# SyncE issues the output weights and the first expert weights after 13 of the 16 ada items of the two summed groups

## The chip, the cores and the metric

The kernel runs on one core of a Trainium2 chip. The metric is device time in microseconds (us), from the first to the last instruction of the program and what lies around it. The kernel before takes 1914.93 us, the median of three runs (1913.94 to 1918.86).

## What is computed

Two blocks run one after the other on 256 tokens of width 1024, all in float32. The first has two layers:

```python
def first_block(x, c, ...):
    cond = silu(c)
    for i in range(2):
        mod = cond @ ada_w[i] + ada_b[i]             # 1024 x 6144: 24 MB of weights per layer
        sh1, sc1, g1, sh2, sc2, g2 = split(mod, 6)
        h = rms_norm(x, norm1_g[i]) * (1 + sc1) + sh1
        y = diff_attention(h, ...) if i == 0 else stick_breaking_attention(h, ...)
        x = x + g1 * y
        h = rms_norm(x, norm2_g[i]) * (1 + sc2) + sh2
        x = x + g2 * hierarchical_moe(h, ...)        # 32 experts, gate, up and down of 2 MB each
    return rms_norm(x, final_norm_g)
```

Each attention has an input product `h @ w_in` (1024 x 3072, six pieces of 2 MB) and an output product `o @ w_out` (two pieces of 2 MB). The second block takes the result and a context through two more layers; its modulation comes from `w_mod_2` in the same way as above.

## The kernel before, in words

**The ring.** SyncE (SP) loads nearly all large weights into a ring of six slots of 2 MB, in one fixed order: for layer `l` the six pieces of the input weights, the two of the output weights (`weight(l, n)`, n = 0 to 7, L1256 to L1269), then gate, up and down of every expert (`expert(l, e)`, L1324 and L1330). Before each load it waits in `room(n)` until the load six places earlier has been used. So the output weights take the slots of the first two input weights, and gate and up of experts 0 and 1 take the slots of the other four; the loads after them need the slots of the output weights. The downs of the first two experts do not lie in the ring in layer 0 and come later, behind another wait (L1284).

**The ada items.** The modulation of both blocks is computed in 64 items, each 1 MB of a modulation matrix: 8 items (one for each eighth of the 1024 rows) make a group of 2048 columns. GpSimd (POOL) loads them, in order, into three buffers (`ada_load`, L1371). Item i is called by its number here; items 0 to 31 are loaded in layer 0, 32 to 63 in layer 1 (32 to 34 a little earlier). Groups 1, 2, 5 and 6 are *summed* (items 0 to 15 and 32 to 47): VectorE (DVE) scales each item by its column of `cond` and adds it to the item before (`ada_sum`, L1699, first item L1701), and TensorE (PE) needs one short product with a column of ones for the eighth item of the group. In the other groups PE multiplies each item itself. The load of item i waits until item i-3 is free: for a summed one that is when item i-2 has been added.

**Counting.** The semaphore `ada_used` counts items in order: DVE raises it for the first seven items of a summed group, PE for all others.

**PE's order.** PE takes the items at fixed places in its program:

```python
QKV_ITEMS = ...                  # item 7 (39) behind step 6 of the input product, item 15 (47) behind step 11, its last
DIFF_ITEMS = share_out(16, [0, 0] + 8 * [1] + [0, 0] + 4 * [1, 0])   # layer 0: items 16 to 23 in steps 2 to 9, ...
if 1 <= k < 9: ada_item(47 + k)  # layer 1: items 48 to 55 in steps 1 to 8 of 18
```

In layer 0, behind item 20 is loaded, POOL also waits until the row of group 2 is stored (`ada_store`, L1389), and issues a bias load, three short column loads and two row loads before it loads item 21; in layer 1 the same stands in front of item 53. After the attention come the output product (`projection`), the router and the experts. In `projection` PE frees the slots of the output weights (L2106), and with that SP goes on.

Of the kernel before, what the change touches and what calls it, by code (L numbers as in the profile page):

```python
# [29 lines left out]
KT = D // P  # L30
# [102 lines left out]
def program(nc, a, out, sb, sem, ctx):  # L133
# [49 lines left out]
    LAST0, LAST1 = 4, 8  # L183
# [143 lines left out]
    def slot(n):  # L327
        return n % RING
# [5 lines left out]
    def free(n):  # L334

        return sem(f"used{slot(n)}")

    def wslot(n, rows_, cols):
        return ring[:, slot(n), :].rearrange("p (t n) -> p t n", t=rows_)[:, :, 0:cols] if cols else None
# [915 lines left out]
    def _(sp):  # L1255
        def room(n):  # L1256

            if n >= RING:
                sp.wait_ge(free(n), n // RING)

        def weight(l, n):

            room(L_BASE[l] + n)
            W = a[loads[l][n]][0]
            if n < 6:
                src = W[:, n * 512:(n + 1) * 512].rearrange("(p t) n -> p t n" if l else "(t p) n -> p t n", t=KT)
            else:
                src = W[:, (n - 6) * 512:(n - 5) * 512].rearrange("(t p) n -> p t n", t=KT)
            sp.dma_start(wslot(L_BASE[l] + n, KT, 512), src).then_inc(sem(f"loaded{slot(L_BASE[l] + n)}"), 16)  # L1269
# [76 lines left out]
        for l in range(2):  # L1346
            for n in range(8):
                weight(l, n)
            for e in range(NX):
                if e == TAIL:  # L1350
                    sp.wait_ge(sem("cnt"), EACH["cnt"] * l + 1)
                    fullest = sp.value_load(most[0:1, 0:1], min_val=0, max_val=S)
                    with sp.If(fullest > LIST):
                        overflow(l)
                expert(l, e)
# [1071 lines left out]
```

## Time and profile before

| | |
|---|---|
| median of 3 runs | 1914.93 us (1913.94 to 1918.86) |
| span of the profiled execution | 1914.1 us; its whole time is not listed apart, and the median lies 0.8 us above this span |
| PE busy | 1697.9 us (89%) |
| DVE busy | 500.2 us (26%) |
| DMA | 586.38 MB, mean 306 GB/s |
| longest chain | PE 54%, DMA 30%, DVE 7% |

Columns of a group of instructions: busy time and mean time of one, then the idle time of the engine before them and what ended most of it. In a timeline a row starts with the start and the duration in us, and the last bracket is the idle time before. q1 is the queue of SP's transfers, q0 that of POOL's; the share of a queue is that of the time of the 16 DMA engines in the stretch. Times are from the start of the span.

### The profile page before, as it was taken

The numbers are of one execution on the slowest core, as the hardware profiler recorded it, in microseconds if no ns is written. First come the engines' busy times: TensorE is split into PE (matmuls) and PEld (weight loads), VectorE is DVE, ScalarE is ACT, GpSimd is POOL, SyncE is SP. The second block draws the span as 40 slices with busy tenths as digits, with TensorE's granted clock in tenths as the row PEclk, the third lists the DMA queues.
The fourth block names the chain that finished last, engine by engine and source line by source line (L and its number), as shares of the span: only waits on it lengthen the run. The fifth ranks groups of instructions, "written<-read, shape, count | busy, mean of one in ns | idle before, by whom it ended". The sixth has DMA issues, their size and how long they took to land.

```text
span 1914.1 us, 18209 instructions
## 1 busy us (share of the span) xinstructions
PE 1697.9 (89%) x7421; PEld 848.8 (44%) x7421; DVE 500.2 (26%) x944; ACT 398.0 (21%) x860; POOL 96.0 (5%) x167
## 2 busy tenths in 40 slices
PE   5967799889898888989989899999999899889988
PEld 3823353333333333845453433333343456555564
DVE  1338331000000103243241000010102334663362
ACT  2003121111111101114231111011100334352351
POOL 1102000000000010123000000000001000000000
PEclk9988899999999989999999999999999899999999
DMA  9997179999999999986369999999999622123310
GB/s 352 389 381 284 45 281 379 422 423 422 423 421 421 421 419 402 379 335 237 115 262 417 424 417 423 418 421 419 419 420 385 237 90 89 57 79 125 111 66 23
DMA packets 122521, 586.38 MB, mean 306 GB/s; under 512 B 10275, under 2 KB 15467, under 8 KB 97849
## 3 DMA queue, kind: packets, MB, share of 16 engines
q1 hardware_dynamic: 99064, 491.94, 63.6%
q0 software_dynamic: 16192, 82.13, 11.5%
q10 hardware_dynamic: 7168, 11.02, 1.5%
q8 instruction: 63, 1.03, 0.2%
q14 instruction: 34, 0.27, 0.0%
HBM read 572.89 MB, written 12.15 MB: 306 GB/s over the span
## 4 chain that ended last, share of the span: by engine, by line
PE 54%; DMA 30%; DVE 7%; ACT 3%; issue 3%; SPq 2%; POOL 0%; ACTq 0%; DVEq 0%
PE psum L2019 51%; DMA ring<-in_expert_w_up 21%; DMA work<-in_ada_w 4%; DMA ring<-in_diff_w_in 2%; DVE work L1699 1%; DMA work<-in_ctx 1%; PE psum L619 1%; DVE small L966 1%; DMA ring<-in_consts 1%; SPq L1324 1%; PE psum L2258 1%; PE psum L1096 1%; SPq L498 1%; DVE work L1911 1%; SPq L1303 0%
## 5 line engine op out<-in xcount | busy, mean ns | idle before, releaser
L2019 PE MATMUL psum<-ring,work 128*64 128x512 f32 (+5 forms) x4432 | 1150.4, 574 | 78.8 <-DMA ring<-in_expert_w_up 64.2
L2019 PEld LDWEIGHTS psum<-ring,work 128*64 128x64 f32 (+2 forms) x4432 | 444.2, 153 | 700.8 <-issue 666.6
L2019 PE MATMUL psum<-work 128*128 128x192 f32 (+8 forms) x920 | 193.5, 378 | 8.1 <-DVE work L1849 4.2
L1911 DVE TENSOR_TENSOR work<-work,psum 128x256 f32<-128x256 f32 x64 | 26.9, 421 | 614.4 <-ACT work L1623 614.4
L2019 PEld LDWEIGHTS psum<-work 128*128 128x128 f32 (+2 forms) x920 | 130.8, 192 | 103.4 <-issue 84.0
L1623 ACT ACTIVATE work<-psum 128x256 f32<-128x256 f32 x64 | 24.5, 383 | 689.1 <-PE psum L2019 689.1
L2019 PE MATMUL psum<-work,ring 128*128 128x256 f32 (+1 forms) x728 | 161.2, 380 | 4.4 <-DMA ring<-in_diff_w_in 1.5
L2019 PEld LDWEIGHTS psum<-work,ring 128*128 128x128 f32 x728 | 136.0, 191 | 29.8 <-issue 7.2
L1502 ACT ACTIVATE work<-psum 128x256 f32<-128x256 f32 (+4 forms) x153 | 69.7, 461 | 229.0 <-PE psum L2258 67.5
L1933 DVE TENSOR_TENSOR work<-psum,rows 128x512 f32<-128x512 f32 x64 | 44.2, 691 | 272.0 <-PE psum L2019 272.0
L1699 DVE SCALAR_TENSOR_TENSOR work<-work,small 128x2048 f32<-128x2048 f32 x28 | 65.8, 2351 | 94.8 <-DMA work<-in_ada_w 94.5
L1502 ACT ACTIVATE ring<-psum 128x512 f32<-128x512 f32 (+3 forms) x82 | 49.9, 608 | 77.0 <-PE psum L2019 56.6
L1571 ACT ACTIVATE work<-psum,small 128x192 f32<-128x192 f32 x128 | 58.4, 506 | 25.2 <-PE psum L2019 25.2
L2019 PE MATMUL psum<-work,cst 128*128 128x256 f32 (+4 forms) x152 | 28.5, 413 | 27.5 <-DVE work L1699 20.0
L1464 POOL DMA_INDIRECT work<-expert_rows,picks x8 | 7.7, 965 | 883.8 <-DMA expert_rows<-work 882.0
L2258 PE MATMUL psum<-cst,work 128*128 128x128 f32 x128 | 28.0, 300 | 17.7 <-DVE work L1911 17.7
L966 DVE TENSOR_REDUCE small<-psum 128x1 f32<-128x512 f32 (+1 forms) x48 | 28.7, 598 | 47.1 <-PE psum L2019 46.9
L619 PE MATMUL psum<-cst 128*128 128x256 f32 x166 | 40.6, 396 | 0.0
L2019 PE MATMUL psum<-work,small 128*2 128x512 f32 (+1 forms) x256 | 37.9, 677 | 2.4 <-DMA work<-in_ada_w 1.8
L839 ACT ACTIVATE ring<-psum,small 128x512 f32<-128x512 f32 (+1 forms) x48 | 29.6, 616 | 41.5 <-DVE small L966 39.8
L1176 PE MATMUL psum<-cst,ring 128*128 128x128 f32 x160 | 27.3, 286 | 11.6 <-DVE ring L972 11.1
L619 PEld LDWEIGHTS psum<-cst 128*128 128x128 f32 x166 | 31.6, 198 | 10.7 <-issue 6.7
(258 smaller groups left out, 817.9 us busy)
## 6 DMA issues: line engine op xcount, KB each, us to landing
ring<-in_expert_w_gate SPq DMA_DIRECT2D x60, 2048.0 KB, 16.7
ring<-in_expert_w_up SPq DMA_DIRECT2D x60, 2048.0 KB, 21.3
ring<-in_expert_w_down SPq DMA_DIRECT2D x57, 2048.0 KB, 21.1
work<-in_ada_w POOLq DMA_DIRECT2D x40, 1024.0 KB, 8.4
ring<-in_w_in SPq DMA_DIRECT2D x12, 2048.0 KB, 9.1
work<-in_w_mod POOLq DMA_DIRECT2D x16, 1024.0 KB, 5.2
ring<-in_diff_w_in SPq DMA_DIRECT2D x6, 2048.0 KB, 37.4
ring<-in_sb_w_in SPq DMA_DIRECT2D x6, 2048.0 KB, 25.0
```

The lines of the kernel that those rows point to most:

```text
L619: nc.tensor.matmul(bank[b][:, 0:S], ident, cst[:, 0:S], start=True, stop=True, skip_group_check=True)
L839: nc.scalar.activation(pe_[:, k % 3, 0:n * P], bank[4 + k % 3][:, 0:n * P], ACT.Exp, bias=nm2[:, k % 3:k % 3 + 1], accum_out=sm2[:, k % 4: ...
L966: V.tensor_reduce(nm2[:, k % 3:k % 3 + 1], bank[4 + k % 3][:, 0:n * P], AX.X, ALU.max, negate=True).then_inc(sem("a_max"), 1)
L1176: ins = T.transpose(bank[(7, 2)[u % 2]][:, j * P:(j + 1) * P], pe_[:, u % 3, j * P:(j + 1) * P], ident)
L1502: copy = lambda o_, i_: nc.scalar.activation(o_, i_, ACT.Copy)
L1571: ins = nc.scalar.activation(hS[:, c // QUAD % 2, t, 0:QUAD * LIST], bank[b][:, k * S:k * S + QUAD * LIST], ACT.Identity, scale=gain[:, t: ...
L1623: nc.scalar.activation(s_act, gu_bank(e)[:, 0:S], ACT.Silu).then_inc(sem("silu"), 1)
L1699: ins = V.scalar_tensor_tensor(now, now, cond[:, 0, t:t + 1], before, ALU.mult, ALU.add)
L1911: V.tensor_tensor(hid, s_act, gu_bank(e)[:, S:2 * S], ALU.mult).then_inc(sem("hid"), 1)
L1933: V.tensor_tensor(outb[:, e % 2, :], bank[5 + e % 2], gate2, ALU.mult).then_inc(sem("out_ev"), 1)
L2019: return T.matmul(out_, lhsT, rhs, start=start, stop=stop, skip_group_check=True)
L2258: ins = T.transpose(bank[2][:, j * P:(j + 1) * P], src[:, j * P:(j + 1) * P], ident)
```

## The change

SP waits once more in each layer, ahead of the first output weight: until 13 items are used in layer 0, and 45 in layer 1 (LAST0 is 4 and KT is 8, so `8 * (4 * l + 2) - 3`).

```diff
         def weight(l, n):

             room(L_BASE[l] + n)
+            if n == 6:
+                sp.wait_ge(sem("ada_used"), KT * (LAST0 * l + 2) - 3)
             W = a[loads[l][n]][0]
```

Everything that SP issues later stands behind this wait: the two output weights, gate and up of experts 0 and 1, and all that follows.

## Rows read from the trace of the kernel before

**Rows 1.** The page: span, and the chain that ended last, by engine.
```profile
span 1914.1 us, 18209 instructions
...
PE 54%; DMA 30%; DVE 7%; ACT 3%; issue 3%; SPq 2%; POOL 0%; ACTq 0%; DVEq 0%
```

**Rows 2.** Waits of the whole span: total, times, longest.
```profile
DVE work L1699 <- DMA work<-in_ada_w: 94.5, 25, 8.8
...
PE psum L2019 <- DVE work L1699: 20.0, 2, 16.4
```

**Rows 3.** Timeline of PE: ends of both input products, and the first output product.
```profile
119.51 7.10 PE L2019 MATMUL psum<-ring,work 128*128 128x512 f32 x16 [0.15 <-PE psum L2019]
143.02 1.89 PE L2019 MATMUL psum<-work,cst 128*1 128x512 f32 x8 [16.41 <-DVE work L1699]
...
211.01 7.13 PE L2019 MATMUL psum<-ring,work 128*128 128x512 f32 x16 [0.69 <-ACT work L1502]
...
854.19 1.04 PE L2019 MATMUL psum<-work,cst 128*1 128x512 f32 x8 [3.56 <-DVE work L1699]
```

**Rows 4.** Timeline of SP: the issues around the change, both layers.
```profile
71.57 15.48 SPq L1269 DMA_DIRECT2D ring<-in_diff_w_out  x2
...
126.65 0.33 SPq L1324 DMA_DIRECT2D ring<-in_expert_w_up  x1
...
778.18 15.79 SPq L1269 DMA_DIRECT2D ring<-in_sb_w_out  x2
806.74 0.34 SPq L1324 DMA_DIRECT2D ring<-in_expert_w_gate  x1
822.26 0.34 SPq L1324 DMA_DIRECT2D ring<-in_expert_w_up  x1
```

**Rows 5.** Windows, two stretches; the last columns are clock, DMA share and GB/s.
```profile
71.60:91.40 19.80, 19.47 (x94) 15.83 (x93) 6.43 (x4) 1.79 (x3) 1.06 (x2) 1.00 1.03 394
...
138.40:164.70 26.30, 16.55 (x99) 6.13 (x100) 22.04 (x50) 8.87 (x38) 8.11 (x15) 0.74 0.80 286
```

**Rows 6.** Waits of SP for the whole span.
```profile
SPq L1324 <- PEq L2106: 112.1, 1, 112.1
```

**Rows 7.** Timeline of POOL: the loads of items 9 and 10, of 41 and 42, of 43.
```profile
91.44 1.74 POOL L1371 DMA_DIRECT2D work<-in_ada_w  x2 [14.26 <-PE psum L2019]
...
815.45 1.74 POOL L1371 DMA_DIRECT2D work<-in_ada_w  x2 [23.21 <-PE psum L2019]
...
823.07 0.55 POOL L1371 DMA_DIRECT2D work<-in_ada_w  x1 [5.30 <-DVE work L1699]
```

**Rows 8.** Items 41 and 42 alone, issued 815 to 817: time to landing.
```profile
DMA to landing us min/median/max: 4.9/6.5/8.1
```

**Rows 9.** Items 11 and 12, issued 102 to 106: time to landing.
```profile
DMA to landing us min/median/max: 11.7/13.7/15.7
```

**Rows 10.** Timeline of DVE: the sums of items 12 and 44.
```profile
121.41 2.35 DVE L1699 SCALAR_TENSOR_TENSOR work<-work,small 128x2048 f32<-128x2048 f32 x1 [4.91 <-DMA work<-in_ada_w]
...
835.24 2.35 DVE L1699 SCALAR_TENSOR_TENSOR work<-work,small 128x2048 f32<-128x2048 f32 x1 [0.15 <-DMA work<-in_ada_w]
```

**Rows 11.** The page, DMA issues: size of each.
```profile
ring<-in_expert_w_gate SPq DMA_DIRECT2D x60, 2048.0 KB, 16.7
...
work<-in_ada_w POOLq DMA_DIRECT2D x40, 1024.0 KB, 8.4
```

**Rows 12.** Timeline of PE: items 21 and 55.
```profile
164.70 1.04 PE L2019 MATMUL psum<-work,small 128*1 128x512 f32 x8 [1.84 <-DMA work<-in_ada_w]
...
890.83 1.04 PE L2019 MATMUL psum<-work,small 128*2 128x512 f32 x8
```

**Rows 13.** Queues in 109.9 to 138.4: packets, MB, share.
```profile
q1 hardware_dynamic: 468, 6.67, 55.1%
q0 software_dynamic: 808, 5.11, 43.8%
```

**Rows 14.** Queues in 112 to 116, when both have work.
```profile
q1 hardware_dynamic: 76, 1.15, 67.5%
q0 software_dynamic: 82, 0.55, 32.7%
```

**Rows 15.** Queue of POOL in 834 to 862.
```profile
q0 software_dynamic: 1136, 5.69, 53.8%
```

**Rows 16.** Queues in 714 to 726, smaller pieces of expert weights beside three items.
```profile
q0 software_dynamic: 368, 2.64, 53.1%
q1 hardware_dynamic: 368, 2.38, 47.9%
```

**Rows 17.** Windows of 5 us at the start of the attention of layer 1.
```profile
850.00:855.00 5.00, 1.44 (x10) 0.11 (x8) 2.35 (x1) 1.88 (x2) 0.00 (x0) 1.00 1.03 429
855.00:860.00 5.00, 2.08 (x13) 1.49 (x10) 2.19 (x5) 2.96 (x6) 2.65 (x5) 0.53 0.97 410
```

**Rows 18.** Timeline of PE: items 48, 49 and 50.
```profile
861.68 1.89 PE L2019 MATMUL psum<-work,small 128*2 128x512 f32 x8
...
868.55 1.20 PE L2019 MATMUL psum<-work,small 128*2 128x512 f32 x8
...
872.40 1.04 PE L2019 MATMUL psum<-work,small 128*2 128x512 f32 x8
```

## The prediction

> **What bounds the kernel now.** I read the page first. The chain that ended last is PE for 54% and DMA for 30% [rows 1], so neither alone bounds the kernel, and the place decides. The view of waits names what the change aims at: PE waited 20.0 us in two places for the summing of ada items on DVE, 16.4 us of it at once, and DVE in turn waited 94.5 us for the items to land [rows 2]. The timeline of PE puts the two places: the input product of layer 0 ends at 126.6 us, and PE stands 16.41 us until item 15 is summed; in layer 1 it stands 3.56 us before item 47 [rows 3]. The timeline of SP shows the competition. The output weights of layer 0 are issued from 71.57 us, and the last of the first expert weights (up of expert 1) at 126.65 us, so six transfers of 2 MB flow beside items 5 to 15 [rows 4]. And the DMA engines are full there: the windows give a share of 1.03 in 71.6 to 91.4, while in 138.4 to 164.7, the first half of the attention, the share is 0.80 [rows 5]. So bytes are what this stage is short of, and the question is whether the change saves bytes ahead of the point that matters, or only moves them.
>
> **The change, part by part.** It adds one wait in each layer and removes nothing. A wait that is met costs a fraction of a microsecond on SP, which is on no chain here. Behind it on SP stand, in each layer, six transfers: two output weights, gate and up of experts 0 and 1. The next one needs the slot that the output product frees, and SP stood 112.1 us for that in layer 0 [rows 6]. So nobody needs the six early: I cost their lateness itself at nothing, covered by the rest of the attention, some 60 us in layer 0. If they landed after 211.01 us they would hold up the output product [rows 3]; by the sums below they land before 170.
>
> *When the wait is met, layer 0.* Items 0 to 8 keep their times, since the group's eighth item has its place in PE's program, behind step 6 of the input product. Loads of items 9 and 10 go out at 91.44 us as before [rows 7]. With no traffic of SP beside them I take layer 1's items 41 and 42, which met almost none: they land 4.9 and 8.1 us after their issue [rows 8], instead of 11.7 to 15.7 us as items 11 and 12 do now [rows 9]. One sum takes 2.35 us [rows 10], a load goes out some 0.3 us after the sum that frees its buffer. Item 9 lands at 96.3 and is summed at 98.7, item 10 at 99.5 and 101.9; item 11 goes out at 99.0, lands 5 us later at 104.0, summed 106.4; item 12 goes out at 102.2, lands 107.2, summed 109.6. That is the thirteenth: SP is released at 109.6 instead of 71.57. Before, the same sum ended at 121.41 + 2.35 = 123.8 [rows 10].
>
> *The wait of 16.41 us.* Item 13 is in flight at 109.6, item 14 just issued, item 15 goes out behind item 13's sum, at about 114.7. Output weights now flow beside them; the nearest row for that has about 8.4 us to landing, as the usual one on the page [rows 11]. So item 15 lands near 123.1 and is summed near 125.5. PE reaches it at 126.6. The wait of 16.41 us is gone, and PE enters the attention at 126.6 instead of 143.0.
>
> *Where the bytes go.* They are now late, and next in line are items 16 to 23, one in each step of the attention. PE took item 21 at 164.70, after 1.84 us of waiting for its landing [rows 12]. Nothing behind that item changes its pace, so its time is the measure of layer 0. The sum is one of engine time. SP still owes 6 x 2.10 MB = 12.6 MB [rows 11]. In 109.9 to 138.4 its queue moved 6.67 MB in 55.1% of 28.5 us, 425 GB/s while it had the engines [rows 13]: 29.6 us. POOL's queue owes items 14 to 21, 8.4 MB, and 0.3 MB of row loads, at 5.11 MB in 43.8% of 28.5 us = 409 GB/s [rows 13]: 21.3 us. If all of SP's goes ahead of item 21, the load of item 21 ends at 109.6 + 29.6 + 21.3 = 160.5. A lone item takes 4.9 us, of which 1.05 MB at 409 GB/s are 2.6, so 2.3 lie around the transfer: it lands at 162.8. **Layer 0: 1.9 us gained**, out of the 16.4.
>
> *Does all of SP's go ahead?* In 112 to 116, with both queues at work, the two moved almost equal numbers of packets, 76 and 82, but 1.15 MB and 0.55 MB [rows 14]: expert weights come in packets twice as large. At one third of the engines, POOL gets only four items through while gate and up of both experts pass. So yes. The Trainium skill says, in "DMA: Bandwidth & Descriptors", section "Queues, rings and completion order", that each engine takes turns between its queues by whole packets, not by bytes; with equal shares of bytes in its place the sum would be rival A's. By that rule, the trace agrees; it speaks against this change.
>
> *Layer 1.* SP issued the output weights from 778.18 us [rows 4]. Now it waits for item 44. Items 41 and 42 go out at 815.45 as before [rows 7] and are summed by 826.5; item 43 (issued 823.07 [rows 7]) without a rival lands at 828.1, summed 830.4, item 44 (issued 826.8) is summed at 834.1, instead of 835.24 + 2.35 = 837.6 [rows 10]. Item 47 then lands near 847 and is summed before PE arrives at 850.6: the 3.56 us are saved. But here SP had issued four of its six transfers by 822.26 [rows 4], in time that was not short, and all six now follow: 12.6 MB, 29.6 us. POOL owes items 46 to 55, the last that stand in consecutive steps: 10.5 + 0.3 MB at 5.69 MB in 53.8% of 28 us = 378 GB/s [rows 15], 28.6 us. 834.1 + 29.6 + 28.6 + 2.3 = 894.6, against 890.83 for item 55 now [rows 12]. **Layer 1: 3.8 us lost**, the saved 3.56 us included.
>
> *Sum.* -1.9 + 3.8 = 1.9 us slower. The span is 1914.1 and the median of the runs 0.8 above it, which I take as what lies around it: 1914.9 + 1.9, about 1917 us. Bounds of the unknown terms: layer 0 between 10.2 us gained (equal shares, rival A) and 1.1 lost, if the engines run at the share of 0.80 of [rows 5] in the last 15 us, where only POOL's loads are left (3 us more); layer 1 between 2.8 us lost and 6.8 lost, by the same two.
>
> **Rival A: POOL keeps half of the engines.** For it: in 714 to 726, beside smaller pieces of expert weights, POOL had 53.1% and moved 2.64 MB against 2.38 [rows 16]. Against it: [rows 14], with the large pieces that flow here. Then layer 0 ends at 109.6 + 21.3 / 0.5 + 2.3 = 154.5, 10.2 us gained; layer 1 at 834.1 + 57.2 + 2.3 = 893.6, 2.8 lost. Sum 7.4 us faster, 1907.5 us.
>
> **Rival B: both waits go and nothing takes their place,** the transfers being hidden in the attention. For it: DMA has a share of 0.80 there [rows 5]. Against it: the free 20% of 26.3 us are 5.3 us of the engines, and SP still owes 29.6 us of them when it is released, of which the rest of the input product covers 17. 20.0 us faster, 1894.9 us.
>
> **Rival C: PE loses its clock in layer 1.** There the attention is PE's own pace, and a stop costs twice. Before, the 3.56 us of waiting and the gap behind them were followed by a granted clock of 0.53, near the lower of its levels of 1.2 and 2.4 GHz [rows 17]; item 48 to item 49 then took 6.9 us where 49 to 50 takes 3.9 [rows 18], 3.0 us lost in a step. If PE stops for each of items 51 to 55, it comes out of the last with two steps at the low clock: 6.0 us on top of the forecast, 1922.9 us. [...] Against it: DMA is the bound up to item 55 anyway, and the full clock may return while it waits. It ends slower than before by more than a measurement tells.
>
> That the wait is met at once and does nothing is excluded in layer 0: SP is at the place at 71.57 and the thirteenth sum is 38 us away, and in layer 1 56 us.
>
> **Chances.** About 0.3%, 5.7 us, is what a measurement of this kernel can tell from no change. The forecast, within that of the time before: 0.47, between 1909 and 1920.6. A: 0.19. B: 0.05, and 0.01 for more. C, and layer 1 at its worse bound with layer 0 at its own: 0.28. So faster 0.25, same 0.47, slower 0.28. The range leaves out B and the tail of C: 1904 to 1925.
>
> **What would show it.** Right: SP issues the output weights near 110 and 834; PE waits under 1 us at item 15 and at item 47; in their place PE waits several times, up to some 6 us each, for landings of items 17 to 21 and 51 to 55; items 17 to 20 need 12 us and more to land; item 21 is taken near 163 and item 55 near 895; the DMA share is close to 1 until 160. The output product starts within 3 us of before in layer 0. Wrong: if item 21 is taken before 157, shares of the queues were mis-sized (A or B); if item 15 is still waited for, the landings beside the output weights were; if the low clock lasts beyond 895, C.

## The result and the profile after

The changed kernel takes 1932.70 us, the median of four runs (1928.85 to 1934.39); the kernel before takes 1916.53 us on the same chip (four runs, 1913.94 to 1918.86). The ratio is 1.0086, 95% interval 1.0070 to 1.0101: slower by some 16 us, where 1917 us had been forecast, 2 us slower. The profiled execution has a span of 1927.0 us, 12.9 more than before; it is the fastest of the four (1928.85), so the rows below hold somewhat less than the 16 us.

The page of the changed kernel, span and busy times; beside [rows 1]:

```profile
span 1927.0 us, 18211 instructions
...
PE 1704.2 (88%) x7421; PEld 850.9 (44%) x7421; DVE 500.2 (26%) x944; ACT 398.2 (21%) x860; POOL 96.0 (5%) x167
```

Timeline of SP: the new wait lets the output weights go at 110.35 and 835.51 us, against 71.57 and 778.18 in [rows 4].

```profile
110.35 0.99 SPq L1271 DMA_DIRECT2D ring<-in_diff_w_out  x2
...
835.51 1.00 SPq L1271 DMA_DIRECT2D ring<-in_sb_w_out  x2
```

Timeline of PE in layer 0: item 15, the items of the first attention steps, and the start of the output product (item 15 and output product of before in [rows 3], item 21 in [rows 12]).

```profile
127.21 1.04 PE L2021 MATMUL psum<-work,cst 128*1 128x512 f32 x8 [0.30 <-PE psum L2021]
...
141.63 1.89 PE L2021 MATMUL psum<-work,small 128*1 128x512 f32 x8 [6.68 <-DMA work<-in_ada_w]
...
149.01 1.88 PE L2021 MATMUL psum<-work,small 128*1 128x512 f32 x8 [3.72 <-DMA work<-in_ada_w]
...
157.62 1.89 PE L2021 MATMUL psum<-work,small 128*1 128x512 f32 x8 [4.31 <-DMA work<-in_ada_w]
...
166.62 1.04 PE L2021 MATMUL psum<-work,small 128*1 128x512 f32 x8 [1.15 <-DMA work<-in_ada_w]
...
212.66 7.13 PE L2021 MATMUL psum<-ring,work 128*128 128x512 f32 x16 [0.69 <-ACT work L1504]
```

The wait of 16.41 us is gone: item 15 follows the input product by 0.30 us. In its place PE waits for items 17, 18 and 19 (6.68, 3.72, 4.31 us) and a little for each up to item 22. Item 21 is taken 1.9 us later than before, and the output product starts 1.65 us later.

The same for layer 1: item 47, then 48, 49, 50, 51 and 55, and the output product. First the output product of the kernel before:

```profile
923.62 7.13 PE L2019 MATMUL psum<-ring,work 128*128 128x512 f32 x16 [0.47 <-ACT work L1502]
```

The changed kernel:

```profile
853.13 1.04 PE L2021 MATMUL psum<-work,cst 128*1 128x512 f32 x8 [0.30 <-PE psum L2021]
...
859.98 1.58 PE L2021 MATMUL psum<-work,small 128*2 128x512 f32 x8
...
871.59 1.89 PE L2021 MATMUL psum<-work,small 128*2 128x512 f32 x8 [7.31 <-DMA work<-in_w_mod]
...
882.71 1.89 PE L2021 MATMUL psum<-work,small 128*2 128x512 f32 x8 [4.29 <-DMA work<-in_w_mod]
...
889.58 1.88 PE L2021 MATMUL psum<-work,small 128*2 128x512 f32 x8
...
905.37 1.04 PE L2021 MATMUL psum<-work,small 128*2 128x512 f32 x8
...
937.87 7.13 PE L2021 MATMUL psum<-ring,work 128*128 128x512 f32 x16 [0.47 <-ACT work L1504]
```

Here is the loss. The wait at item 47 is gone too, but PE takes item 50 at 882.71, 29.6 us after item 47, where before 18.2 us lay between them (854.19 [rows 3], 872.40 [rows 18]). The output product of layer 1 starts 14.25 us later than before, 12.6 of them made in layer 1. And from item 50 on, PE no longer waits for any landing: it runs at its own pace, at first at half its clock (granted clock 0.50 in 882.7 to 889.5, 1.00 in 894.3 to 905): items 50 to 51 take 6.9 us, 51 to 52 take 4.7, later steps 3.7. The loss by rows: PE takes item 50 10.3 us later than before, of which 1.65 come from layer 0; items 50 to 55 take 22.7 us instead of 18.4, 4.2 more; behind item 55 0.3 are won back.

### The profile page after: what moved, and what is told of

The parts are those of the page before. It is cut to its first block, busy times and chain, and to the rows that moved or that the text cites. A ratio compares the mean times of both kernels' runs of the same rounds, so it can differ in the third digit from the quotient of the medians.

```text
span 1927.0 us, 18211 instructions
## 1 busy us (share of the span) xinstructions
PE 1704.2 (88%) x7421; PEld 850.9 (44%) x7421; DVE 500.2 (26%) x944; ACT 398.2 (21%) x860; POOL 96.0 (5%) x167
## 4 chain that ended last, share of the span: by engine, by line
PE 58%; DMA 28%; DVE 6%; ACT 3%; issue 3%; SPq 2%; POOL 0%; ACTq 0%; DVEq 0%
PE psum L2021 54%; DMA ring<-in_expert_w_up 21%; DMA ring<-in_diff_w_in 2%; DMA work<-in_w_mod 2%; DMA work<-in_ada_w 2%; DMA work<-in_ctx 1%; DMA ring<-in_consts 1%; DVE small L966 1%; PE psum L2260 1%; PE psum L1096 1%; PE psum L619 1%; DVE work L1913 1%; SPq L1305 1%; SPq L498 1%; ACT work L1625 1%
## 5 line engine op out<-in xcount | busy, mean ns | idle before, releaser
L1504 ACT ACTIVATE ring<-psum 128x512 f32<-128x512 f32 (+3 forms) x82 | 49.9, 608 | 77.0 <-PE psum L2021 56.6
L1573 ACT ACTIVATE work<-psum,small 128x192 f32<-128x192 f32 x128 | 58.4, 506 | 24.7 <-PE psum L2021 24.7
L839 ACT ACTIVATE ring<-psum,small 128x512 f32<-128x512 f32 (+1 forms) x48 | 29.6, 617 | 41.6 <-DVE small L966 39.9
L1176 PE MATMUL psum<-cst,ring 128*128 128x128 f32 x160 | 27.4, 287 | 11.7 <-DVE ring L972 11.2
L1176 PEld LDWEIGHTS psum<-cst,ring 128*128 128x128 f32 x160 | 19.3, 144 | 34.8 <-DVE ring L972 27.1
## 6 DMA issues: line engine op xcount, KB each, us to landing
ring<-in_expert_w_up SPq DMA_DIRECT2D x60, 2048.0 KB, 21.3
```

The source lines that it names most:

```text
L839: nc.scalar.activation(pe_[:, k % 3, 0:n * P], bank[4 + k % 3][:, 0:n * P], ACT.Exp, bias=nm2[:, k % 3:k % 3 + 1], accum_out=sm2[:, k % 4: ...
L1176: ins = T.transpose(bank[(7, 2)[u % 2]][:, j * P:(j + 1) * P], pe_[:, u % 3, j * P:(j + 1) * P], ident)
L1504: copy = lambda o_, i_: nc.scalar.activation(o_, i_, ACT.Copy)
L1573: ins = nc.scalar.activation(hS[:, c // QUAD % 2, t, 0:QUAD * LIST], bank[b][:, k * S:k * S + QUAD * LIST], ACT.Identity, scale=gain[:, t: ...
```

## The experiments

Each is compared with the kernel before, run beside it. Theory T, formed from these lines: what counts is which of SP's bytes are in POOL's way while an attention takes its items, and the item that is latest against PE's own pace decides.

### Each layer alone

```diff
-            if n == 6:
+            if n == 6 and l == 0:        # the other run: l == 1
                 sp.wait_ge(sem("ada_used"), KT * (LAST0 * l + 2) - 3)
```

> The new wait in layer 0 alone, at 13 used items; layer 1 as before. In the changed kernel the output product of layer 0 starts at 212.66 us against 211.01, 1.65 us late, and most of the loss (12.3 us between there and the output product of layer 1) lies in layer 1. Theory T (bytes of SP pushed ahead of POOL's items; the item that lands last relative to PE's own pace decides): 1 to 3 us slower than before, ratio 1.001. Rival R1 (the change in timing of layer 0 upsets the expert stage, not the attention of layer 1): 8 us or more slower.

> The new wait in layer 1 alone, at 45 used items. Theory T: 12 to 14 us slower than before, ratio about 1.0065; item 50 is waited for and taken some 29 us after item 47, as in the changed kernel (853.13 to 882.71), and item 55 some 52 us after it, against 36.6 before. Rival R1: within 3 us of before.

Layer 0 alone: 1.0017 (1.0000 to 1.0033), 1920.09 us. Layer 1 alone: 1.0065 (1.0035 to 1.0094), 1928.20 us. Layer 1 is as theory T had it; layer 0 loses 3.3 us by the ratio, at the edge of the 1 to 3 expected, and its interval reaches from nothing to 6 us. The layers add up within the intervals (0.17% and 0.65%, against 0.86% together), and R1 falls: in the trace of layer 0 alone the output product of layer 0 starts 4.67 us later than before (215.68) and that of layer 1 5.28 us (928.90), so nearly nothing is added between them. It also shows how far single executions differ: the changed kernel has the same layer 0 and starts that product 3.0 us sooner (212.66). Timeline of PE with layer 1 alone: items 47, 50, 51, 55.

```profile
852.71 1.04 PE L2021 MATMUL psum<-work,cst 128*1 128x512 f32 x8 [0.37 <-DVE work L1701]
...
883.32 1.89 PE L2021 MATMUL psum<-work,small 128*2 128x512 f32 x8 [4.86 <-DMA work<-in_w_mod]
...
890.19 1.89 PE L2021 MATMUL psum<-work,small 128*2 128x512 f32 x8
...
906.11 1.04 PE L2021 MATMUL psum<-work,small 128*2 128x512 f32 x8
```

From item 47 to item 55 PE needs 53.4 us, against 36.6 before (854.19 [rows 3] to 890.83 [rows 12]).

### The first expert weights only behind the attention

```diff
                 weight(l, n)
+            sp.wait_ge(sem("ada_used"), (28, 62)[l])
             for e in range(NX):
```

> The changed kernel with one more wait on SP behind the two output weights: gate and up of experts 0 and 1 are issued only when 28 (layer 0) and 62 (layer 1) items are used, that is when the attention has taken all of its own. Nothing is computed otherwise. Theory T: the items of the attention then meet only the 4 MB of output weights; both waits (16.4 and 3.6 us) stay away and nothing takes their place, and PE keeps its clock at the start of both attentions: 15 to 24 us faster than before, ratio about 0.99. The 8 MB of expert weights flow in the stretch of the output product, in which the engines had stood still (205 to 240). Rival R2 (POOL's loads are slow in the attention for a reason of their own, its latency and three buffers, not because of SP's transfers): the waits for items 17 to 23 and 49 and 50 stay, and it is within 5 us of before or slower. Rival R3 (expert weights late in their own stage): experts 0 and 1 are waited for, 10 us or more given back there.

0.9878 (0.9846 to 0.9910), 1893.39 us: 23 us faster than before, and nearly 40 faster than the changed kernel, by one more wait on the same queue. (The changed kernel and this one were not run side by side; each has its ratio to the kernel before.) Timeline of PE: items 15, 17 and 21, and the first product of the experts.

```profile
127.05 1.04 PE L2022 MATMUL psum<-work,cst 128*1 128x512 f32 x8 [0.47 <-DVE work L1702]
...
135.52 1.89 PE L2022 MATMUL psum<-work,small 128*1 128x512 f32 x8 [0.58 <-DMA work<-in_ada_w]
...
149.17 1.89 PE L2022 MATMUL psum<-work,small 128*1 128x512 f32 x8 [2.44 <-DMA work<-in_ada_w]
...
255.35 7.09 PE L2022 MATMUL psum<-ring,work 128*64 128x512 f32 x32 [1.00 <-ACT work L1574]
```

Item 21 is taken 17.5 us earlier than with the change alone. R2 falls: without SP's transfers beside them POOL's loads are nearly in time, and item 21 alone is still waited for by 2.44 us. R3 falls: the first product of the experts waits for ACT by 1.00 us, as it did before (at 268.91), and for no weights.

### Is the change's own wait part of that gain?

The same without it: the output weights go out as before.

> Without the wait of the change: the output weights go out as before, and only gate and up of experts 0 and 1 wait until 28 and 62 items are used. Theory T: the output weights alone are 4 MB of the 12 that ran beside items 8 to 15, and they are through before item 11, so item 15 is summed before or within 3 us of PE's arrival in layer 0 and before it in layer 1; nothing flows beside the attention. 17 to 24 us faster than before, within 3 us of the run with both waits. Then the wait that the change adds is not what that run gains by. Rival: the hold of the output weights is needed, and a wait of 5 us or more stands at item 15 again.

0.9883 (0.9862 to 0.9904), 1894.20 us: the same as with it, within the intervals. The timeline of PE shows item 15 without a wait here too, behind an input product that ends at 128.5 us (126.6 before).

```profile
128.78 1.04 PE L2020 MATMUL psum<-work,cst 128*1 128x512 f32 x8 [0.30 <-PE psum L2020]
```

So the 16.41 us were made by the 8 MB of expert weights, not by the 4 MB of output weights, and the wait on the output weights brings nothing once the expert weights are out of the way. Holding both longer:

```diff
+            if n == 6:
+                sp.wait_ge(sem("ada_used"), (24, 56)[l])
...
+            sp.wait_ge(sem("ada_used"), (28, 62)[l])
```

> Output weights at 24 and 56 used items, gate and up of experts 0 and 1 at 28 and 62. Theory T: the short waits left in the attention of layer 0 (0.6 and 2.4 us) and at item 47 (1.1 us) go, and nothing new comes, since the 4 MB land in 10 us and the output product starts 33 us after the release: 0 to 4 us faster than with the output weights at 13 and 45, 20 to 27 us faster than before. Rival: the output product waits for its weights, and it is slower than that run.

0.9872 (0.9853 to 0.9891), 1893.17 us: no difference to the last two can be told. The wait of 2.4 us at item 21 stayed (2.28 us), so that part of the expectation was wrong: SP has nothing in flight there, and the wait is no matter of its transfers. What makes it was not tested; the store and the row loads that POOL issues ahead of item 21 are the candidate. Both holds in layer 1 alone:

```diff
+            if n == 6 and l == 1:
+                sp.wait_ge(sem("ada_used"), KT * (LAST0 * l + 2) - 3)
...
+            if l:
+                sp.wait_ge(sem("ada_used"), 62)
```

> Both waits (45 for the output weights, 62 for gate and up) in layer 1 alone. Theory T: 2 to 5 us faster than before, the stall of 3.56 us at item 47 and little else; the other 14 us or more of the run with both layers lie in layer 0. Against the run with the change's wait in layer 1 alone it differs only in when 8 MB of expert weights go out: 15 to 20 us between the two. Rival (the loss in layer 1 is made by holding back the output weights): it stays at 10 us slower or more.

0.9968 (0.9955 to 0.9980), 1909.61 us, 6 us faster than before by the ratio: a little more than expected. The steps of the attention show why: item 48 to item 49 takes 4.3 us (857.05 to 861.31) against 6.9 in [rows 18], because PE, without the stop at item 47, is back at its full clock sooner: the granted clock is 0.67 in 855 to 860 and 1.00 in 860 to 865, against 0.53 and 0.50 before. Against the run with the change in layer 1 alone it is 19 us, by the time at which 8 MB go out and nothing else.

### The expert weights at the time of the change

```diff
+            sp.wait_ge(sem("ada_used"), (13, 45)[l])
             for e in range(NX):
```

> Output weights as before, gate and up of experts 0 and 1 held until 13 and 45 items are used. Theory T: SP owes 8.4 MB instead of 12.6 MB when it is released, 10 us of engine time less in each layer. Layer 0: item 15 in time, items 17 to 19 late, together 5 to 10 us gained. Layer 1: item 50 some 10 us earlier than in the run with the change in layer 1 alone, so 1 to 5 us lost. Sum: 0 to 9 us faster than before. If instead the number of transfers held back does not matter, it is as slow as the changed kernel.

0.9999 (0.9983 to 1.0015), 1917.90 us: no change, at the slow edge of what was expected (0 to 9 us faster), and not by the path expected. Timeline of PE, item 15 and item 47:

```profile
135.78 1.88 PE L2020 MATMUL psum<-work,cst 128*1 128x512 f32 x8 [10.03 <-DVE work L1700]
...
854.88 1.89 PE L2020 MATMUL psum<-work,cst 128*1 128x512 f32 x8 [6.21 <-DVE work L1700]
```

Item 15 is waited for 10 us and item 47 6 us: gate and up of the first expert now go out at 114.23 and 114.62, straight ahead of item 15 (119.70). In the changed kernel the output weights stood between, and beside them items 14 to 16 take 7.9 to 8.2 us to land.

### Smaller pieces of the same bytes

```diff
+                if l and e < 2:
+                    w = a[name][l, e].rearrange("(p t) n -> p t n", p=P)
+                    for q in range(4):
+                        done = sem(f"loaded{slot(n0 + j)}") if q == 3 else sem("quarters")
+                        sp.dma_start(wslot(n0 + j, KT, 512)[:, 2 * q:2 * q + 2, :], w[:, 2 * q:2 * q + 2, :]).then_inc(done, 16)
+                    continue
...
+                if l and e == 0:
+                    pe.wait_ge(sem("quarters"), 12 * 16)
```

> The new wait in layer 1 alone, with gate and up of experts 0 and 1 of layer 1 each loaded as four transfers of 512 KB, whose contiguous pieces are 4 KB and not 16 KB; the bytes are the same. If the queues take turns by packets (theory T), POOL's share beside them rises from about 0.2 to about 0.5, item 50 is taken some 10 us sooner after item 47 than in the run of layer 1 alone, and it is only 0 to 6 us slower than before. If they share by bytes, or the landings are late for another reason, it is as slow as the run of layer 1 alone, 12 us or more.

1.0054 (1.0036 to 1.0072), 1924.91 us. The queues in 852 to 876, first with layer 1 alone, then in small pieces:

```profile
q1 hardware_dynamic: 907, 7.75, 77.5%
q0 software_dynamic: 664, 2.43, 25.2%
```

```profile
q1 hardware_dynamic: 1705, 5.73, 60.2%
q0 software_dynamic: 1144, 4.04, 42.3%
```

With pieces of 4 KB POOL's share rises from 25.2% to 42.3%, and item 50 is taken 17.5 us after item 47 instead of 30.6. The bytes are the same in both, so a sharing by bytes is excluded. The counts of packets say it directly, in 4 us in which both queues have work: in 868 to 872, 98 and 100 with layer 1 alone (1.36 and 0.34 MB), 225 and 224 in small pieces (0.79 and 0.85 MB); in the changed kernel, in 866 to 870:

```profile
q1 hardware_dynamic: 97, 1.33, 78.4%
q0 software_dynamic: 96, 0.39, 23.9%
```

So with SP's pieces at 4 and at 16 KB the queues take turns packet by packet. It does not hold beside the output weights, whose packets are of 2 KB: in 116 to 122 of the changed kernel the counts are 575 and 173 (1.15 and 1.29 MB), and POOL has 51.7% of the engines. So the output weights leave POOL half and the expert weights a quarter or less, at these sizes. What sets the turn for small packets was not tested.

In whole time the small pieces are hardly better (1.0054 and 1.0065 cannot be told apart): the bytes still owed now stop PE at item 53, while the last of SP's bytes come through (0.20 MB in 890 to 892, 0.04 in 892 to 894):

```profile
869.13 1.04 PE L2027 MATMUL psum<-work,small 128*2 128x512 f32 x8
...
889.57 1.89 PE L2027 MATMUL psum<-work,small 128*2 128x512 f32 x8 [6.60 <-DMA work<-in_w_mod]
```

The share says where the wait falls; the bytes owed say that there is one.

### The clock's part in layer 1

```diff
+                if k in (2, 3):
+                    keep_warm(5, (24, 30)[k - 2])        # second run: (12, 15)
                 if 1 <= k < 9:
                     ada_item(47 + k)
```

> The run with the change's wait in layer 1 alone, with 24 and 30 filler products on PE ahead of items 49 and 50 (products of constants into an unused bank, their result is not read), so that PE stays busy where it waited 6 and 5 us and worked at half its clock. Theory T with the clock as a part of the loss: item 50 lands as late as there (some 30 us after item 47), but the two steps behind it take 3.7 us each instead of 6.9 and 4.9, so item 55 comes some 4 us earlier; about 4 us faster than that run, 8 us slower than before, ratio about 1.004. Rival (the clock follows from something else, or the landing of item 50 is itself later because of the fillers): no faster than that run.

1.0073 (1.0049 to 1.0098), 1932.61 us. The fillers were twice as long as meant, and PE came late to both items by itself; it says nothing on the clock but that the steps behind them then took 3.7 us. By the timeline the two blocks took 10.6 and 13.2 us; the 10.8 in the text that follows is wrong. Hence the second:

> As the run with fillers before, with half as many (12 and 15): there one filler took 0.22 us twice, the two blocks 10.6 and 10.8 us, twice what was meant, so that PE came late to items 49 and 50 by itself. Now the blocks take 5.3 and 6.6 us and should end inside the waits. Theory T: item 50 is taken some 30 us after item 47 as in the run of layer 1 alone, the steps behind it take 3.7 us each, and item 55 comes 49 us after item 47 instead of 53.4: about 4 us faster than that run. Rival: the same time as that run, within 2 us, in the distance from item 47 to item 55.

1.0059 (1.0040 to 1.0077), 1925.62 us. Timeline of PE: items 47, 50, 51, 55.

```profile
850.39 1.04 PE L2021 MATMUL psum<-work,cst 128*1 128x512 f32 x8 [0.86 <-DVE work L1701]
...
881.00 1.04 PE L2021 MATMUL psum<-work,small 128*2 128x512 f32 x8 [0.81 <-DMA work<-in_w_mod]
884.68 1.04 PE L2021 MATMUL psum<-work,small 128*2 128x512 f32 x8
...
900.26 1.04 PE L2021 MATMUL psum<-work,small 128*2 128x512 f32 x8
```

Item 50 comes 30.6 us after item 47, as without fillers, and item 55 49.9 us after it instead of 53.4: the low clock costs 3.5 us of the loss. The steps behind item 50 now run at a granted clock of 1.00, with one wait of 0.76 us for item 53 among them, which is why it is 3.5 here and 4.2 in the rows of the changed kernel. In whole time the two runs cannot be told apart (1.0059 and 1.0065); the trace shows it, the timing does not.

## Why the prediction was wrong

**Right:** the forecast of where SP goes on (109.6 and 834.1, measured 110.35 and 835.51), that both waits go, that what takes their place are waits for landings in the attention, that all of SP's bytes pass ahead of items 21 and 55 (its last ones by 160 and 882), and that layer 1 loses more than layer 0. While the expert weights flow, POOL has 29.1% of the engines in layer 0 (128 to 155) and 21.8% in layer 1 (852 to 876).

**The step that failed** is the measure of layer 1: "POOL owes items 46 to 55, the last that stand in consecutive steps", set against the time of item 55. It had PE wait for landings at items 51 to 55; PE waited at items 49 and 50 (7.31 and 4.29 us) and at none behind them. The sum of engine time was good, but for another item. It holds up to the one that lands when SP's last byte is through; from there POOL loads an item in 2.8 us (1.05 MB at 378 GB/s), while PE takes one every 3.7 us (item 50 to item 55 before, [rows 18] and [rows 12]). So behind that item PE is the slower of the two, and its own pace must be added.

For item 50 the prediction's own terms give 834.1 + 29.6 + 5 x 2.8 + 2.3 = 880.0; with layer 1 alone, where SP was released at 836.1, they give 882.0 and the trace says 883.32. Then five steps of 3.7 us lead to 898.5, 7.7 us behind the 890.83 of before, instead of the 3.8 forecast. The other part is the clock, which the forecast put at nothing and left to rival C: 3.5 us by the second run with fillers. Together 11.2 us of the 12.6 that layer 1 lost; most of the last 1.4 is item 50 itself, which comes 1.3 us later than the same sum gives from either release (883.32 for 882.0, 882.71 for 881.4), and why is open; single executions of one stage can differ by that much (3.0 us in layer 0, above). This pricing was made after the runs, and only on layer 1.

**Rival C had the clock's part in kind, and not the rest.** It had two slow steps behind the last wait, at 3.0 us each; they came behind item 50 and cost 3.2 and 1.0. It held "DMA is the bound up to item 55 anyway" against it, which is the same error. What it lacked was PE's five full steps behind item 50.

**Layer 0** was mis-sized by 3.8 us: item 21 at 166.62 instead of 162.8. The queues of the changed kernel from the release to that item:

```profile
q1 hardware_dynamic: 2656, 12.58, 55.1%
q0 software_dynamic: 1596, 10.09, 46.5%
```

SP's 12.6 MB are right, at 31.0 us of engine time (forecast 29.6); POOL moved 10.09 MB at 26.2 us, not 8.7 MB at 21.3, since the rest of item 13 and the loads behind item 21 (items 22 and 23 went out at 159.84 and 164.46) share the engines. The sum comes to 57.2 us for a stretch of 56.3. The gain of 1.9 us was a loss of 1.65 in this trace, and of 4.67 in that of layer 0 alone.

**Rival A** would have needed POOL to hold its share. Small pieces came near to giving it, and from item 47 (851.64) to the output product (932.04) PE then took 80.4 us, against 86.0 in the run of layer 1 alone and 69.4 before. So a third of that loss went: a better share only moves the wait to a later item. **Rival B**, with nothing in the place of the two waits, came true only where the 8 MB of expert weights left the attention: 23 us faster, where B had 20.0.

**What the prediction did not ask** is which of the six transfers make the wait of 16.41 us. It treated them as one lot. The expert weights did it, and they are the ones that no one needs before 255 us, even in the fastest of these kernels.

## What to carry to other kernels

When loads are held back to let others pass, give the released bytes a place where nothing else flows; here the engines stood still during the output product (their share is 0.00 in 205 to 240 us, before and with the change), and the change let the bytes go at 110. To price bytes that come late, go through the items one by one: landing by engine time up to each, plus the consumer's own pace from there to the end, and take the largest. That fits layer 1 here within some 1.4 us, after the fact, and has not been tried as a forecast. Hold back first the transfer that is needed last, not the next one in the queue.

## What the runs showed of the hardware

A transfer of a few KB can take as long as the large ones issued before it on its queue: in layer 1 of the changed kernel the store of a row of 8 KB, issued at 856.58, landed 26.3 us later, 0.2 us behind the last half of item 50, issued 0.5 us ahead of it. POOL stood 8.28 us for it, which PE did not feel.

```profile
883.13 2.15 POOL L1381 DMA_DIRECT2D rows<-in_b_mod  x4 [8.28 <-DMA mod_scratch<-rows]
```

Landings beside the expert weights take long: items 19 and 20 needed 24.7 and 19.2 us, where the longest in the kernel before, in that stretch, was 15.7 [rows 9].
